# Wider row groups for the expert gate and up pieces, with the chunks of an expert taken in pairs

## The reference, cut to what matters

```python
D_MODEL = 1024; SEQ = 256; N_EXPERTS = 8; TOP_K = 2; D_FF_EXPERT = 3584; MOE_BLOCK = 128

def swiglu(h, w_gate, w_up, w_down):
    return (jax.nn.silu(h @ w_gate) * (h @ w_up)) @ w_down

def moe_swiglu(h, router_w, w_gate, w_up, w_down):
    ...                          # top-2 router, rows sorted by expert into blocks of 128
    def expert_block(args):
        xb, e = args
        return swiglu(xb, w_gate[e], w_up[e], w_down[e])
    yb = lax.map(expert_block, (buf.reshape(n_blocks, MOE_BLOCK, D), block_exp))
    ...                          # rows go back to their tokens, times the gates
```

## Time and profile before

| | before |
|---|---|
| median of three runs | 1400.8 us |
| the profiled execution's own time | 1401.09 us |
| its span, first to last instruction | 1398.8 us |
| TensorE busy | 1379.2 us, 99% |
| VectorE busy | 1137.6 us, 81% |
| ScalarE busy | 933.0 us, 67% |
| moved by DMA | 448.78 MB, mean 321 GB/s |

### The profile page before, as it was taken

One profiled execution on the slowest core, in us unless ns is written; L12 is line 12 of the kernel. 1 busy time (PEld: TensorE's weight loads), 2 busy tenths in 40 slices (PEclk: granted clock), 3 DMA queues, 4 the chain that ended last, 5 costly groups with the idle time before them and its releaser, 6 DMA issues.

```text
span 1398.8 us, 19126 instructions
## 1 busy us (share of the span) xinstructions
PE 1379.2 (99%) x7313; PEld 1172.1 (84%) x7313; DVE 1137.6 (81%) x872; ACT 933.0 (67%) x751; POOL 35.8 (3%) x53
## 2 busy tenths in 40 slices
PE   9999999999999999999999999999999999999986
PEld 8888999889888888888888888888888888888765
DVE  6866565556857998988888888898888888888897
ACT  5555443445645777777777777777777777777775
POOL 0010000000010020000000000000000000000200
PEclk9999999999999999999999999999999999999998
DMA  9734985546424999999999999999999999999993
GB/s 333 278 106 152 398 321 182 197 164 204 157 92 149 350 371 395 396 394 397 387 394 395 356 385 394 373 370 387 391 357 395 389 370 375 394 389 351 397 394 153
DMA packets 191039, 448.78 MB, mean 321 GB/s; under 512 B 8516, under 2 KB 11275, under 8 KB 190987
## 3 DMA queue, kind: packets, MB, share of 16 engines
q1 hardware_dynamic: 189162, 441.74, 86.1%
q0 software_dynamic: 1616, 5.77, 1.1%
q10 hardware_dynamic: 208, 0.54, 0.1%
HBM read 429.67 MB, written 18.36 MB: 320 GB/s over the span
## 4 chain that ended last, share of the span: by engine, by line
PE 88%; DVE 5%; DMA 3%; issue 1%; ACT 1%; SPq 1%; DVEq 0%; ACTq 0%
PE ps L551 81%; DVE w_lo L386 4%; DMA raw<-in_expert_w_up 2%; PE ps L1010 2%; ACT w_hi L381 1%; PE ps L682 1%; DMA raw<-in_w_in 1%; PE ps L713 0%; PE ps L969 0%; PE ps L736 0%; PE ps L640 0%; PE ps L671 0%; PE ps L556 0%; PE ps L935 0%; PE ps L980 0%
## 5 line engine op out<-in xcount | busy, mean ns | idle before, releaser
L386 DVE TENSOR_TENSOR w_lo<-raw,w_hi 128x2048 fp32r<-128x2048 f32 x401 | 914.5, 2290 | 186.7 <-ACT w_hi L381 186.0
L381 ACT ACTIVATE w_hi<-raw 128x2048 fp32r<-128x2048 f32 x400 | 766.4, 1918 | 296.5 <-PE ps L551 276.4
L551 PE MATMUL ps<-w_hi,xe_hi 128*128 128x512 f32 x896 | 244.8, 395 | 0.0
L551 PE MATMUL ps<-w_lo,xe_hi 128*128 128x512 f32 x896 | 240.1, 390 | 0.1
L551 PE MATMUL ps<-w_hi,xe_lo 128*128 128x512 f32 x896 | 240.0, 390 | 0.0
L551 PEld LDWEIGHTS ps<-w_hi,xe_lo 128*128 128x128 f32 x896 | 168.2, 188 | 35.9
L551 PEld LDWEIGHTS ps<-w_lo,xe_hi 128*128 128x128 f32 x896 | 167.9, 188 | 36.2 <-DVE w_lo L386 0.9
L551 PEld LDWEIGHTS ps<-w_hi,xe_hi 128*128 128x128 f32 x896 | 164.6, 188 | 31.7
L551 PE MATMUL ps<-w_lo,he_hi 128*128 128x512 f32 x448 | 121.4, 392 | 5.7 <-DVE w_lo L386 5.5
L551 PE MATMUL ps<-w_hi,he_hi 128*128 128x512 f32 x448 | 121.1, 391 | 0.5 <-DVE he_hi L1921 0.5
L551 PEld LDWEIGHTS ps<-w_lo,he_hi 128*128 128x128 f32 x448 | 83.4, 188 | 26.4 <-DVE w_lo L386 9.3
(11 more groups left out here) (264 smaller groups left out, 964.1 us busy)
## 6 DMA issues: line engine op xcount, KB each, us to landing
raw<-in_expert_w_gate SPq DMA_DIRECT2D x112, 1024.0 KB, 7.5
raw<-in_expert_w_up SPq DMA_DIRECT2D x112, 1024.0 KB, 7.7
raw<-in_expert_w_down SPq DMA_DIRECT2D x112, 1024.0 KB, 7.4
raw<-in_w_in SPq DMA_DIRECT2D x23, 1024.0 KB, 6.0
raw<-in_dense_w_gate SPq DMA_DIRECT2D x11, 1024.0 KB, 6.4
raw<-in_dense_w_up SPq DMA_DIRECT2D x11, 1024.0 KB, 7.2
raw<-in_dense_w_down SPq DMA_DIRECT2D x11, 1024.0 KB, 5.0
raw<-in_w_out SPq DMA_DIRECT2D x8, 1024.0 KB, 5.8
```

The lines of the kernel that those rows point to most:

```text
L381: nc.scalar.activation(half_of(w_hi, n), raw[:, n % RAW, :], ACT.Copy).then_inc(hi_ready, 1)
L386: nc.vector.tensor_tensor(half_of(w_lo, n), raw[:, n % RAW, :], half_of(w_hi, n).bitcast(F32), ALU.subtract).then_inc(lo_ready, 1)
L551: return pe.matmul(o, stationary, moving, start=start, stop=stop, skip_group_check=True)
```

## The change

The gate and up weights are cut in another way. Chunks 0 to 5 are taken in three pairs (E_PAIRS = 3). A pair has four gate pieces and four up pieces, each of two row groups by 1024 columns, so that the run of a source row is 4 KB. Chunk 6 is worked on alone, with pieces as before. Within a wide piece the matmuls alternate between the pair's two banks, with the same stationary operand twice in a row.

The order of the pieces is then: gate 0/1 (4), up 0/1 (4); gate 2/3, up 2/3, down 0 and 1 (4); gate 4/5, up 4/5, down 2 and 3; gate 6 (2), up 6 (2), down 4 and 5 (4); down 6 (2). There are still 42 pieces and the same 504 matmuls in a full block.

The small steps come two at a time. Both chunks of a pair are turned one after the other, into banks 7 and 6. `silu` no longer waits for the up product. Both multiplications into `hid` follow each other on VectorE, and so do the two of `he_lo`. In the first block `gates` and `block_list` both stand between the low parts of piece 7 and piece 8, `destinations` between those of 15 and 16. In the last block the first `add_rows` stands before the second down piece of chunk 2, the second before the second down piece of chunk 3, and the other two after that piece.

The order of pieces and the loads:

```diff
         def expert_pieces():
             order = []
-            for c in range(E_CH + 1):
-                if c < E_CH:
-                    order += [("gate", c, 0), ("gate", c, 1), ("up", c, 0), ("up", c, 1)]
-                if c > 0:
-                    order += [("down", c - 1, 0), ("down", c - 1, 1)]
+            for p in range(E_PAIRS + 1):
+                for kind in ("gate", "up"):
+                    order += [(kind, p, i) for i in range(pieces_in(p))]
+                if p > 0:
+                    order += [("down", c, h) for c in (2 * p - 2, 2 * p - 1) for h in range(2)]
+            order += [("down", E_CH - 1, h) for h in range(2)]
...
-                        src = (egate_v if kind == "gate" else eup_v)[e, :, 4 * h:4 * h + 4, c * CH:c * CH + CH]
+                        view = egate_v if kind == "gate" else eup_v
+                        if c < E_PAIRS:
+                            src = view[e, :, 2 * h:2 * h + 2, 2 * c * CH:2 * c * CH + 2 * CH]
+                        else:
+                            src = view[e, :, 4 * h:4 * h + 4, 2 * c * CH:FE]
```

TensorE, within a piece and over a block:

```diff
+                    if p < E_PAIRS:
+                        parts = [(2 * i + k, o, 2 * k * CH + o * CH) for k in range(2) for o in range(2)]
+                    else:
+                        parts = [(4 * i + k, 0, k * CH) for k in range(4)]
+                    for k, o, at in parts:
+                        add(ps[:, bank + o, :], xe_hi[:, k, :], hi[:, at:at + CH], start=(k == 0))
...
+                for p in range(E_PAIRS + 1):
+                    if p > 0:
+                        pe.wait_ge(esilu_done, b * E_CH + 2 * p)
+                    for i in range(pieces_in(p)):
+                        expert_in("gate", p, i)
+                    if p > 0:
+                        turn_hidden(2 * p - 2)
+                        if p == 1 and last_block:
+                            pe.wait_ge(hot_saved, 1)
+                        turn_hidden(2 * p - 1)
...
+                    if p == E_PAIRS and not last_block:
                         turn_gathered(b)
...
+                    for i in range(pieces_in(p)):
+                        expert_in("up", p, i)
...
+                    if p > 0:
+                        down(2 * p - 2, 0)
+                        down(2 * p - 2, 1)
+                        down(2 * p - 1, 0)
+                        if p == E_PAIRS:
+                            turn_hidden(E_CH - 1)
+                        down(2 * p - 1, 1)
```

ScalarE, over a pair:

```diff
+                    hi_of("up", p, 0)
+                    hi_of("up", p, 1)
+                    if p > 0:
+                        hidden_hi(2 * p - 2)
+                        hidden_hi(2 * p - 1)
+                    if p < E_PAIRS:
+                        hi_of("up", p, 2)
+                        silu(2 * p)
+                        hi_of("up", p, 3)
+                        silu(2 * p + 1)
+                    if first and p == 0:
                         scale_rows()
```

VectorE, over a pair:

```diff
+                        lo_of("gate", p, i)
+                        if p == 1 and i == 1:
+                            hidden(0)
+                            hidden(1)
...
+                    lo_of("up", p, 0)
+                    lo_of("up", p, 1)
+                    if p > 0:
+                        hidden_lo(2 * p - 2)
+                        hidden_lo(2 * p - 1)
+                    if p < E_PAIRS:
+                        lo_of("up", p, 2)
...
+                        lo_of("up", p, 3)
+                    if first and p == 0:
+                        gates()
+                    if first and p == 1:
+                        destinations()
+                    if p > 0:
+                        lo_of("down", 2 * p - 2, 0)
+                        if last_block and p == 2:
+                            add_rows(0, 0)
+                        lo_of("down", 2 * p - 2, 1)
+                        if p == E_PAIRS:
+                            hidden(E_CH - 1)
                         else:
...
+                            hidden(2 * p)
+                            hidden(2 * p + 1)
+                        lo_of("down", 2 * p - 1, 0)
+                        if last_block and p == 2:
+                            add_rows(0, 1)
+                        lo_of("down", 2 * p - 1, 1)
+                    if last_block and p == 2:
                         for t in range(TT):
...
+                            add_rows(1, t)
+                    if first and p == 0:
                         block_list()
```

More of the change, by code:

```diff
@@ L1009, in turn_hidden @@
                     for f in range(4):
[L1010 removed]
+                        last = pe.transpose(ps[:, 7 - c % 2, f * P:f * P + P], hid[:, c % 2, f * P:f * P + P], ident)
                     last.then_inc(et_done, 1)
@@ L1063, in down_by_columns @@
                             last.then_inc(y_first, 1)
[L1065 to L1071, removed]
+                down = few_down if last_block else expert_down
+                for p in range(E_PAIRS + 1):
[8 more added lines that the diff above has]
+                        turn_hidden(2 * p - 1)
+                    if p == 0 and last_block:
                         pe.wait_ge(last_hot, 1)
@@ L1352, in silu @@
                 def silu(c):
-                    act.wait_ge(piece_used, nth(MOE0 + AT[("up", c, 1)] + 1, b))
+                    act.wait_ge(piece_used, nth(MOE0 + AT[last_in("gate", c)] + 1, b))
                     nc.scalar.activation(sil[:, c % 2, :], ps[:, c % 2, :], ACT.Silu).then_inc(esilu_done, 1)
[L1356 to L1369, removed]
-                    else:
[L1371 to L1382, removed]
-                        scale_rows()
-                    if c == E_CH and not last_block:
-                        gathered(b + 2)
@@ new lines, in hidden_hi @@
+                def hidden_hi(c):
+                    act.wait_ge(et_done, b * E_CH + c + 1)
+                    if last_block:
+                        copy(he_hi[:, c % 2, :, 0:FEW],
+                             ps[:, 7 - c % 2, :].rearrange("p (f r) -> p f r", r=P)[:, :, 0:FEW]).then_inc(eh_hi, 1)
+                    else:
+                        copy(both(he_hi[:, c % 2]), ps[:, 7 - c % 2, :]).then_inc(eh_hi, 1)
+                for p in range(E_PAIRS + 1):
+                    for i in range(pieces_in(p)):
+                        hi_of("gate", p, i)
+                        if p == 0 and i == 1 and not first:
+                            output_rows(b)
+                    hi_of("up", p, 0)
[9 more added lines that the diff above has]
+                    if first and p == 0:
+                        scale_rows()
+                    if p > 0:
+                        hi_of("down", 2 * p - 2, 0)
+                        if p == E_PAIRS:
+                            silu(E_CH - 1)
+                        hi_of("down", 2 * p - 2, 1)
+                        hi_of("down", 2 * p - 1, 0)
+                        hi_of("down", 2 * p - 1, 1)
@@ L1387, in _ @@
+                hi_of("down", E_CH - 1, 0)
+                hidden_hi(E_CH - 1)
+                hi_of("down", E_CH - 1, 1)
+                if not last_block:
+                    gathered(b + 2)
             gathered(1)
@@ L1940, in expert_block @@
                         block_list()
-                    if first and c == 3:
-                        destinations()
-                    if first and c == 4:
+                    if first and p == 1:
                         rows_before_last()
-                    if first and c == 5:
+                    if first and p == 2:
                         few_columns()
-                    if last_block and c in (4, 5):
-                        for t in range(TT):
-                            add_rows(c - 4, t)
```

114 lines of the change are left out of this document (50 added, 64 removed).

## The result

Fifteen executions of each kernel, taken together: 1403.69 us in the median after the change (1401.63 to 1404.47), 1400.56 before it (1398.36 to 1403.54). The ratio is 1.0019, with a 95% interval of 1.0011 to 1.0027. The predicted time was 1402.6 us, its range 1399.0 to 1406.0. Two later comparisons of the same two kernels gave 1.0015 (1.0006 to 1.0024) both times, with medians 2.3 and 2.0 us apart.

What follows compares the result with a forecast made beforehand. TensorE was taken to bound the six middle blocks, leaving room only in the first and last. Terms 0 + 2.1 - 0.3 = +1.8 us on 1401.09 gave 1402.9, as a median 1402.6 us; range 1399.0 to 1406.0.

Steps and rivals of the forecast that it cites:

- The bound: Six of the eight blocks run at TensorE's own pace, 118.51 us; room for gain or loss only in first and last.
- Matmuls: Wide pieces: 504 matmuls alternating between two banks cost nothing; half a nanosecond either way is 1.2 us for the range.
- Steady blocks, 0: Six middle blocks: paired small steps use up nobody's spare time, cost 0; 0.6 us in all if the cover fails.
- what the prediction itself called wrong: Signs against it: steady blocks off by over 0.2 us, a clock under 1.00 in them, or a last block under 113 us.
- The covers that I named: Steady blocks: 2.8 us of spare time before low parts, turns many pieces after their inputs, gathered rows asked for early enough.
- First block, +2.1: Block 0: joined router lists stall TensorE 2.3 us at piece 8, with smaller waits later, less 0.55 for a vanished stall.
- the walk: Piece-by-piece count of VectorE's lateness against 2.8 us spare time, 0.51 regained a piece; 2.3 us stall at piece 8.
- Last block, -0.3: Last block: 114.2 us by VectorE's lateness alone against 114.5 before, with wide pieces' faster landing removing the DMA's loss.
- credited the wide runs with 3.6 us: Last block: 24 wide gate and up pieces landing at 2.56 us rather than 2.71 save 3.6 us.
- The 3.5 us of DMA: Last block of the kernel before: 3.5 of the 9.4 us lost come from late weight loads that ScalarE waited for.
- The clock: Rival: alternating banks take TensorE's clock down to 0.93 over the wide pieces, price 39 us, 1440; chance 0.02.
- The sum: Whole kernel: 0 + 2.1 - 0.3 = +1.8 us against the profiled execution's 1401.09, median 1402.6 us.

Runs made afterwards that it cites:

- the narrow and the wide kernels: Narrow: the changed kernel with gate and up pieces back at 2 KB runs, 1402.98 us; wide: the changed kernel itself, 1402.38 us beside it.

## Why the prediction was right, point by point

- **The bound.** TensorE's pace in the steady blocks: right in every trace. Room only in the first and the last block: not quite, since TensorE's own pace had 0.2 us a block to give.
- **Matmuls.** No change from alternating banks: right, the narrow and the wide kernels have the same 118.31 us. The Trainium skill's rule in "TensorE: Matmul & The Clock Gate", section "A second HAM failure mode: psum-queue depth-cycling", does not show here: steady blocks, whose groups follow each other without a wait, have a clock of 1.00.
- **Steady blocks, 0.** Mis-sized: -1.2 us in all, 0.20 a block, just short of what the prediction itself called wrong (over 0.2). I asked what two small steps side by side would cost on VectorE and ScalarE and missed what two turns side by side save on TensorE, 0.2 us a block. The covers that I named did hold: TensorE waits for nobody in blocks 1 to 6.
- **First block, +2.1.** Measured +2.0 in the trace of after, with the wait at the low matmuls of piece 8 that the walk put at 2.3. The bracket says 2.22; by the starts of the groups it is 2.37 (467.41 less 464.13, less the usual 0.91).
- **Last block, -0.3.** Measured 0.0. The walk's waits were 0.6, 0.4, 1.4, 1.7 and 2.1; the three long ones are 1.29, 1.50 and 1.92 in the brackets of the trace and 1.46, 1.67 and 2.08 by the starts of the groups, each with 0.1 of slow start behind it. But the reason given for the vanished DMA cost was wrong. I credited the wide runs with 3.6 us; narrow runs in the same order cost nothing either. The 3.5 us of DMA in the kernel before was right (3.4, or 2.7 against another trace), its cure was the order. That the term came out near zero was luck: for wide pieces that land no faster the prediction had the last block up to 2 us longer, and narrow ones cost nothing.
- **The clock.** Here the prediction failed by omission. It tied a fall to the alternating banks, at 2%, and let the new waits cost only their length. By the estimate above the falls cost some 1.3 us more on average over the executions. Traces of before didn't show it: the wait of 3.01 us in the earlier trace rows has the clock at 1.00 around it.
- **The sum.** +1.8 forecast, +3.1, +2.3 and +2.0 measured. Two errors of opposite sign cancelled in it, the 1.2 us that the steady blocks gave and the some 1.3 us that the clock took, so the closeness of the number is in part luck. The 1.1 us by which the first median, 1403.69, lies above 1402.6 are not explained; the later medians are 1402.38 and 1402.82.

What stays open: why the same wait takes the clock down in one execution and not in the next, and why a longer one in the kernel before did not; what moves the start of the experts by 2 us between executions, what the 0.3 us after the last block are, and what part of the median's 3.1 us in the first comparison is chance, since the later two gave 2.3 and 2.0.

## What to carry to other kernels

Where a bound engine is fed by another that has a fixed spare time, write that spare time down (here 2.8 us, regained at 0.5 a piece) and place every extra piece of work by it; two lists that cost nothing apart, placed together, cost block 0 2.0 us, more than the 1.2 us that the pairs saved in the steady blocks. When two traces differ by less than the two medians do, look at the granted clock of each execution, take a second trace, and compare the kernels block by block. Faster landings are worth nothing where another engine's lateness covers them; halving the bytes of one stage shows whether they matter, if the clock is the same in both traces.

## What the runs showed of the hardware

- A wait of TensorE of about 2 us, in a stretch otherwise filled with matmuls, was followed by about 3 us at the lower clock level in four of seven traces, and by none in the other three. It cost 1.2 us in block 0, on top of the wait. Three waits of 1.3, 1.5 and 1.9 us within 10 us were followed by the same fall in three of eight traces, at 1.5 to 1.6 us. A single wait of 3.0 us elsewhere was not, in two traces. With matmuls of the identity in the wait of block 0 none of three traces has the fall, and one of 33 executions has a mean clock of 0.994 or less, against 18 of 37.
- After a group of transposes the first group of matmuls is followed by the next after 1.0 us in place of 0.91. Three such places fewer in a block, with the transposes themselves unchanged, came with 0.2 us less.
- Loads of 1 MB land every 2.71 us with runs of 2 KB and every 2.56 us with runs of 4 KB when the DMA engines are full, also where the runs lie 14 KB apart.
